# Last feed-forward's gate and up products as seven quarter-block products instead of eight, with GpSimd forming the weight sums

## The chip, the cores and the metric

The kernel runs on one core of a Trainium2 chip. The metric is the device time of one execution in microseconds (us). Five queues work side by side: TensorE (PE in the profile; its weight loads are listed apart as PEld), VectorE (DVE), ScalarE (ACT), GpSimd (POOL) and SyncE (SP), which here only issues transfers. They meet in semaphores.

## What is computed

Two transformer blocks run one after the other over 512 tokens of width 1024, all in float32. The change touches only the last part of the second block, its second feed-forward:

```python
h = modulate(x, norm_g[l, 2], mod[:, 2, 0], mod[:, 2, 1])      # rms norm, gain, shift
x = x + 0.5 * mod[:, 2, 2][:, None, :] * swiglu(h, ffn2_w1[l], ffn2_w3[l], ffn2_w2[l])

def swiglu(h, w1, w3, w2):                                     # 1024 -> 2816 -> 1024
    return (jax.nn.silu(h @ w1) * (h @ w3)) @ w2
```

## The kernel before, in words

Activations lie transposed: a tile is 128 features (partitions) by 512 tokens (columns), so `X` is 8 tiles of the model width and the inner width of 2816 is 22 tiles. A float32 product is made of three products of the shorter type float32r: each operand is split into a high part (a rounded copy, by ScalarE) and a low part (operand minus high part, by VectorE), and TensorE accumulates high x high, high x low and low x high in one bank of PSUM (`split_product`, lines 499 to 501). Every such matmul has its own weight load.

Weights come in chunks of 128 x 1024 (512 KB) in the fixed order of `STREAM`. Chunk n goes through `RAW[n % 3]` (transfer, SP), `HI[n % 3]` (line 1204, ScalarE, semaphore `hi_ready`) and `LO[n % 3]` (line 1693, VectorE, `lo_ready`); TensorE counts `chunk_used` when it is done with one. SP starts the transfer of chunk n+3 when the low part of chunk n is made.

In a feed-forward (`ffn` on each engine) a chunk of gate or up weights is one tile of the inner width: 8 blocks of 128 x 128, 24 matmuls of 512 columns. Tile 0 is computed by `unrooted` from x times gain before the norm's factor is known, and scaled afterwards; tile 1 by `behind`, block by block as the norm's tiles appear (lines 607 to 611); the other 20 tiles are 40 chunks in a row. ScalarE takes the silu of the gate out of PSUM (line 1598), VectorE multiplies it with the up product (line 2404), and the hidden tile is split again (`HIDH`, line 1605; `HIDL`, line 2409). When all 22 hidden tiles are there, the down projection runs: 8 output tiles, each three chunks of 8, 8 and 6 blocks, 528 matmuls in all, each output tile added into `X` by VectorE (line 2464) and stored.

The order on each engine is written out by hand. GpSimd issues transfers and does a few copies earlier in the kernel and has nothing in this stage. Memory of the stage: `HIDH` and `HIDL` take 44 KB per partition each.

Of the kernel before, what the change touches and what calls it, by code (L numbers as in the profile page):

```python
# [15 lines left out]
P = 128  # L16
# [31 lines left out]
def swapped(half):  # L48
# [11 lines left out]
          ("out2", 8), ("up3", 2 * FT), ("down3", 3 * DT))  # L60
# [6 lines left out]
LAST_DOWN = [8, 8, 6]  # L67

# [3 lines left out]
def build(nc, wst, ada, cond_d, xT, cols_d, squares_d, pos1_d, pos2_d, lams_d, out):  # L72
    ctx = ExitStack()
    with ctx:
# [49 lines left out]
        HIDL = at("HIDL", A0 + 44, [P, FT, S], F32R)  # L124

# [121 lines left out]

        UP_FIRST = SQ[:, 0, :]
# [8 lines left out]
        def normed(k, t):  # L257
            return Y2[:] if k == 1 and t == 2 else Y[:, t % 2, :]
# [141 lines left out]
        def _(sp):  # L400
# [19 lines left out]
            repeat(sp, (NCH - 3) // 3, more)  # L420
            for n in range(3 + (NCH - 3) // 3 * 3, NCH):
                sp.wait_ge(sem("lo_ready"), n - 2)
                sp.dma_start(RAW[n % 3][:], wst[n]).then_inc(sem(f"raw{n % 3}"), 16)
# [52 lines left out]


        @block.tensor
        def _(pe):
# [32 lines left out]
            def warm_up(n):  # L512

                pe.wait_ge(sem("warm_set"), 1)
                for _ in range(n):
                    mm(PS[:, 5, :], Y[:, 1, 0:P], Y[:, 1, :], start=True, stop=True)
# [311 lines left out]
            def latent_work():  # L828
# [54 lines left out]
                for j in range(3):  # L883
# [3 lines left out]
                    for r in range(2):  # L887
                        to = bank_for(f"uq{2 * j + r}")
                        ins = split_product(to, w, range(3 * r, 3 * r + 3), range(3), (LQH, LQL))
                        if r:  # L890
                            used(ins)
                        else:
                            ins.then_inc(sem("uq_half"), 1)
# [7 lines left out]
                for m in range(4):  # L901
# [3 lines left out]
                    else:  # L905
                        ins.then_inc(sem("uk_done"), 1)
# [3 lines left out]
                for b in range(NB):  # L910
# [9 lines left out]
                    else:  # L920
                        ins.then_inc(sem("uv_done"), 1)
# [237 lines left out]

            warm_up(3)  # L1160
# [22 lines left out]
            ffn(2, 6)  # L1183
# [3 lines left out]
        def _(act):  # L1187
            A = nc.scalar.activation

            def split_hi(n0, step=0, i=0):  # L1190
# [6 lines left out]
                if step == 0:  # L1197
                    act.wait_ge(sem(f"raw{n0 % 3}"), 16 * (n0 // 3 + 1))
# [31 lines left out]
            def load_roots():  # L1230

                A(SM[:, 85:86], EPSC, ACT.Sqrt).then_inc(sem("table_loaded"), 1)

            def stds(k):
                if k == 4:
                    act.wait_ge(sem("fused_sums"), 2)
                    A(FSTD[:, 0:4], FV[:, 0:4], ACT.Sqrt, bias=EPS2C, scale=1.0 / D).then_inc(sem("fused_std"), 1)
# [8 lines left out]
            def high(k, t):  # L1246
# [8 lines left out]
                else:  # L1255
                    shift = 3 * g * DT + t
                    A(oh[:, t, :], Y[:, t % 2, :], ACT.Identity, bias=MOD[:, shift:shift + 1])\
                        .then_inc(sem("split_hi"), 1)

            def norm(k):  # L1260
# [20 lines left out]
                for t in range(nt):  # L1281
# [5 lines left out]
                    if t == 5:  # L1287
                        split_hi(NEXT[k] + 2)

            def unrooted_copy(k, r):  # L1290
# [4 lines left out]
                else:  # L1295
                    A((SILU[0], UP_FIRST)[r], PS[:, r, :], ACT.Copy).then_inc(sem("unrooted_copied"), 1)

            def table(k, tab):

                act.wait_ge(sem("angle"), k + 1)  # L1300
                A(tab[:, 1, :], Y[:, 0, :], ACT.Sin).then_inc(sem("sin"), 1)
# [23 lines left out]
            def project_in2():  # L1325
                n0 = FIRST["in2"]
                for j in range(IN2_STEPS):
                    if j > 2:
                        split_hi(n0 + j)
                    if j == IN2_STEPS - 1:  # L1330

                        A(SM[:, 85:86], EPSC, ACT.Exp).then_inc(sem("table_loaded"), 1)
# [63 lines left out]
            def latent_copies(p):  # L1396
# [12 lines left out]
                if 12 <= p < 18:  # L1409
# [3 lines left out]
                    else:  # L1413
                        act.wait_ge(sem("uq_half"), m // 2 + 1)
# [1288 lines left out]
```

## Time and profile before

| | |
|---|---|
| Time, median of 3 runs | 1868.12 us (1867.55 to 1869.95) |
| Span of the profiled execution, first to last instruction | 1863.9 us |
| TensorE matmul records / weight load records | 1855.8 us / 1488.2 us |
| VectorE / ScalarE / GpSimd busy | 1071.2 / 742.6 / 60.0 us |
| Last feed-forward, after its norm, to the end | 1523 to 1864 us |

The profiled execution is given by its span alone; the runs' times also hold what lies before its first and after its last instruction, and their median is 4.2 us above it. A matmul's record runs from its start to its last result, and records of neighbours overlap, so TensorE's sum of records says only that it has no pauses; what one matmul costs is the distance between two starts.

### The profile page before, as it was taken

The page shows a single profiled execution, that of the slowest core. Times are in us where ns is not written, and L with a number is a line of the kernel's source. Part 1 is how long each engine was busy: PE and PEld are TensorE (multiplying, and loading weights), DVE is VectorE, ACT ScalarE, POOL GpSimd, SP SyncE. Part 2 cuts the span into 40 slices and gives each one's busy share as a digit, 9 for nine tenths or more (in the row PEclk, how much of TensorE's full clock was granted, in tenths as well). Part 3 has the DMA queues.
Part 4 walks back from the last instruction along what each step waited for, and adds up shares of the span by engine and source line. Part 5 has one row for each costly group of instructions (what it writes and reads, how often), then busy time and mean ns, then how long its engine had stood idle before and what let it go on. Part 6 is the DMA issues. An engine that isn't in the chain of part 4 may idle for free.

```text
span 1863.9 us, 24687 instructions
## 1 busy us (share of the span) xinstructions
PE 1855.8 (100%) x8814; PEld 1488.2 (80%) x8816; DVE 1071.2 (57%) x1755; ACT 742.6 (40%) x1251; POOL 60.0 (3%) x104
## 2 busy tenths in 40 slices
PE   9999999999999999999999999999999999999999
PEld 7777778888888888888888888767768888888887
DVE  7777456757666566733334457867785773333332
ACT  6465445442223233432323334456555452232221
POOL 0001000001111000000000010100000000000000
PEclk9999999999999999999999999999999999999999
DMA  5212213447777563333232332211112333333332
GB/s 187 90 57 68 66 59 121 135 140 227 233 217 226 186 207 111 91 98 101 90 101 91 113 102 91 81 57 54 50 57 68 102 91 102 91 100 97 96 112 90
DMA packets 58285, 207.71 MB, mean 111 GB/s; under 512 B 6688, under 2 KB 6816, under 8 KB 58208
## 3 DMA queue, kind: packets, MB, share of 16 engines
q1 hardware_dynamic: 47232, 167.67, 28.6%
q0 software_dynamic: 10976, 39.00, 6.7%
q8 instruction: 50, 0.82, 0.2%
q14 instruction: 27, 0.22, 0.0%
HBM read 204.48 MB, written 2.10 MB: 111 GB/s over the span
## 4 chain that ended last, share of the span: by engine, by line
PE 97%; DVE 2%; issue 1%; ACT 0%; DVEq 0%; ACTq 0%
PE PS L499 27%; PE PS L501 27%; PE PS L500 27%; PE PS L996 2%; PE PS L1036 2%; PE PS L1023 1%; PE PS L607 1%; PE PS L608 1%; PE PS L611 1%; PE PS L535 1%; PE PS L652 1%; PE PS L539 1%; PE PS L536 1%; PE PS L943 1%; PE PS L768 1%
## 5 line engine op out<-in xcount | busy, mean ns | idle before, releaser
L1693 DVE TENSOR_TENSOR LO<-RAW,HI 128x1024 fp32r<-128x1024 f32 x309 | 377.9, 1223 | 396.3 <-ACT HI L1204 394.4
L499 PE MATMUL PS<-XH,HI 128*128 128x512 f32 x1424 | 561.9, 395 | 0.0
L501 PE MATMUL PS<-XH,LO 128*128 128x512 f32 x1424 | 554.9, 390 | 0.0
L500 PE MATMUL PS<-XL,HI 128*128 128x512 f32 x1424 | 554.4, 389 | 0.0
L1204 ACT ACTIVATE HI<-RAW 128x1024 fp32r<-128x1024 f32 x309 | 326.6, 1058 | 521.7 <-PE PS L501 507.1
L499 PEld LDWEIGHTS PS<-XH,HI 128*128 128x128 f32 x1424 | 267.3, 188 | 61.6 <-issue 7.8
L501 PEld LDWEIGHTS PS<-XH,LO 128*128 128x128 f32 x1424 | 267.3, 188 | 56.9
L500 PEld LDWEIGHTS PS<-XL,HI 128*128 128x128 f32 x1424 | 267.5, 188 | 53.4
L499 PE MATMUL PS<-HIDH,HI 128*128 128x512 f32 x528 | 205.4, 389 | 0.0
L500 PE MATMUL PS<-HIDL,HI 128*128 128x512 f32 x528 | 205.4, 389 | 0.0
L501 PE MATMUL PS<-HIDH,LO 128*128 128x512 f32 x528 | 205.4, 389 | 0.0
L500 PEld LDWEIGHTS PS<-HIDL,HI 128*128 128x128 f32 x528 | 99.1, 188 | 20.7
L501 PEld LDWEIGHTS PS<-HIDH,LO 128*128 128x128 f32 x528 | 99.1, 188 | 20.6
L499 PEld LDWEIGHTS PS<-HIDH,HI 128*128 128x128 f32 x528 | 99.1, 188 | 20.5
L1874 DVE SCALAR_TENSOR_TENSOR ADA<-ADA,COND 128x1024 f32<-128x1024 f32 x72 | 87.8, 1220 | 20.8 <-DMA ADA<-ada 20.4
L2404 DVE TENSOR_TENSOR Y<-T,PS 128x512 f32<-128x512 f32 x43 | 29.6, 689 | 82.1 <-PE PS L501 82.1
L2223 DVE TENSOR_REDUCE SM<-PS 128x1 f32<-128x128 f32 (+3 forms) x96 | 43.8, 487 | 31.8 <-issue 15.5
L1598 ACT ACTIVATE T<-PS 128x512 f32<-128x512 f32 x28 | 16.7, 597 | 96.4 <-PE PS L501 96.4
L1605 ACT ACTIVATE HIDH<-Y 128x512 f32 (+1 forms) x66 | 41.7, 632 | 22.9 <-DVE Y L2404 21.1
L1510 ACT ACTIVATE P<-PS,SM 128x128 f32<-128x128 f32 (+3 forms) x64 | 33.2, 524 | 43.5 <-DVE SM L2223 43.4
L499 PE MATMUL PS<-MH,HI 128*128 128x512 f32 x128 | 49.8, 389 | 0.0
L500 PE MATMUL PS<-ML,HI 128*128 128x512 f32 x128 | 49.8, 389 | 0.0
(408 smaller groups left out, 2123.9 us busy)
## 6 DMA issues: line engine op xcount, KB each, us to landing
RAW<-weights SPq DMA_DIRECT2D x309, 512.0 KB, 3.5
ADA<-ada POOLq DMA_DIRECT2D x72, 512.0 KB, 4.6
y_out<-X SPq DMA_DIRECT2D x8, 256.0 KB, 4.7
X<-x_in SPq DMA_DIRECT2D x3, 512.0 KB, 7.4
RAW<-weights SPq DMA_DIRECT2D x4, 256.0 KB, 5.2
X<-x_in SPq DMA_DIRECT2D x2, 256.0 KB, 4.0
COND<-condition POOLq DMA_DIRECT2D x1, 512.0 KB, 4.7
SQC<-squares SPq DMA_DIRECT2D x1, 320.0 KB, 8.5
```

The lines of the kernel that those rows point to most:

```text
L499: mm(bank, a, moving[0][:, t, :], start=start, stop=False)
L500: mm(bank, a, moving[1][:, t, :], start=False, stop=False)
L501: ins = mm(bank, z, moving[0][:, t, :], start=False, stop=stop)
L996: mm(PS[:, score_bank(a, u), 0:n], at_["q"](2 * p + r, i), at_["k"](2 * p + r, n), start=True, stop=False)
L1036: ins = mm(PS[64 * r:64 * r + 64, 5 + g % 2, k * P:(k + 1) * P], ATT[a]["v"](kb, 2 * p + r), ATT[a]["PT"][2 * (t % 2) + r][:, kb * P:(kb + ...
L1204: A(HI[n0 % 3][:], RAW[n0 % 3][:], ACT.Copy).then_inc(sem("hi_ready"), 1)
L1510: A(at_["P"][u % 3][:, 0:n], PS[:, score_bank(a, u), 0:n], ACT.Exp, bias=NMX[:, u % 4:u % 4 + 1], accum_out=RSU[:, u % 4:u % 4 + 1]).then_ ...
L1605: A(HIDH[:, bass.ds(t, 1), :], Y[:, 0:1, :], ACT.Copy).then_inc(sem("hid_hi"), 1)
L1693: V.tensor_tensor(LO[n0 % 3][:], RAW[n0 % 3][:], HI[n0 % 3][:].bitcast(F32), ALU.subtract)\
L1874: V.scalar_tensor_tensor(out=ADA[j][:], in0=ADA[j][:], scalar=1.0, in1=COND[:], op0=ALU.mult, op1=ALU.mult, accum_out=MOD[:, bass.ds(step ...
L2223: V.tensor_reduce(NMX[:, u % 4:u % 4 + 1], PS[:, score_bank(a, u), 0:n], AX, ALU.max, negate=True)\
L2404: V.tensor_tensor(Y[:, 0, :], SILU[j % 3], PS[:, 2 * (j % 3) + 1, :], ALU.mult)\
```

## The change

**Products.** Twenty pairs replace the 40 chunks: an even pair p holds the gate weights of two inner tiles, an odd one the up weights of the same two. A pair's weights are a 2 x 2 block matrix (contraction halves by the two tiles: a11, a12, a21, a22, each 128 x 512 in memory), the normed tokens are one as well (feature tiles 0 to 3 and 4 to 7 by tokens 0 to 255, `EARLY`, and 256 to 511, `LATE`). Instead of eight products of quarter blocks there are seven (the form with four weight sums and four token sums): `A11 A12 S1 S2 S4 S3 A22`, each 4 blocks x 3 = 12 matmuls of 256 columns. The order is `A11 A12` of pair 0 and then for every p: `S1 S2 S4 A11(p+1) S3 A12(p+1) A22`. Products are accumulated on each other in PSUM where the scheme allows it (S2 on A11's bank, S4 on S1's, S3 and A22 on A11's); three intermediate results per pair are copied out by ScalarE and three added by VectorE.

**Weights.** The pairs' weights go to a new ring of two buffers (`SRAW`, two transfers of 512 KB each). GpSimd makes the four sums S1 = a21 + a22, S2 = S1 - a11, S4 = a12 - S2, S3 = a11 - a21 into `SB`. Each of the seven forms (512 columns) is split into high and low parts in the old `HI` and `LO` buffers, four products ahead; two forms that are neighbours in one buffer and ready together are split by one instruction of 1024 columns, others singly.

**Tokens.** Four sums T1 to T4 of the normed tokens (1024 columns each) and their high and low parts are made once, by GpSimd, VectorE and ScalarE together, at the start of the stage.

**Order.** The inner width is worked off in three parts of 8, 8 and 6 tiles (6, 8 and 6 pairs), each followed by its share of the down projection over all 8 output tiles, added into `X` every time. In the last part the last product stands behind the first blocks of the down projection. Tile 0's scaling and tile 1's product on VectorE and ScalarE are moved in between the products.

**Queues.** While TensorE works on product s, ScalarE and VectorE each go through one step, in this order. `after_product(s - 1)`: ScalarE copies the result of A11, S1 or S2 (and takes the silu of A22's in an even pair); VectorE adds to the result of A12, S4 or S3 and in an odd pair multiplies with the silu. `ahead_hi` and `ahead_lo`: the high and the low part of a form four products ahead. `later`: silu of the sums in an even pair, the hidden tile's high or low part in an odd one.

**Elsewhere.** Some semaphores are merged or dropped to make room (`uq_half`, `uk_done`, `uv_done` become `latent_part`; table loads and half copies no longer increment anything).

```diff
-          ("out2", 8), ("up3", 2 * FT), ("down3", 3 * DT))
+          ("out2", 8), ("up3", 4), ("fa3", 22), ("da3", 8), ("fb3", 28), ("db3", 8), ("fc3", 20), ("dc3", 8))
+def _products():
+    order = [("A11", 0), ("A12", 0)]
+    for p in range(NPAIRS):
+        order += [("S1", p), ("S2", p), ("S4", p)]
+        order += [("A11", p + 1)] * (p + 1 < NPAIRS) + [("S3", p)]
+        order += [("A12", p + 1)] * (p + 1 < NPAIRS) + [("A22", p)]
+    return order
...
SP
+            def pair(p, m):
+                if p < 2:
+                    sp.wait_ge(sem("branch_scaled"), 2 * DT)
+                else:
+                    sp.wait_ge(sem("s_made"), 4 * p - 4)
+                    sp.wait_ge(*low_made("A22" if m else "A12", p - 2))
+                sp.dma_start(SRAW[p % 2][:, m, :], wst[real_pair(p, m)]).then_inc(sem(f"sraw{p % 2}{m}"), 16)
...
GpSimd
+            def sums_of(p):
+                w = SRAW[p % 2]
+                a11, a12, a21, a22 = w[:, 0, 0:S], w[:, 0, S:2 * S], w[:, 1, 0:S], w[:, 1, S:2 * S]
+                pool.wait_ge(sem(f"sraw{p % 2}1"), 16 * (p // 2 + 1))
+                if p:
+                    pool.wait_ge(*low_made("S1", p - 1))
+                pool.tensor_tensor(SB[:, 0, :], a21, a22, ALU.add).then_inc(sem("s_made"), 1)
...
+                pool.tensor_tensor(SB[:, 1, :], SB[:, 0, :], a11, ALU.subtract).then_inc(sem("s_made"), 1)
...
+                pool.tensor_tensor(SB[:, 2, :], a12, SB[:, 1, :], ALU.subtract).then_inc(sem("s_made"), 1)
...
+                pool.tensor_tensor(SB[:, 3, :], a11, a21, ALU.subtract).then_inc(sem("s_made"), 1)
+            def token_sums():
+                pool.wait_ge(sem("normed"), NDB[6] + 4)
+                pool.tensor_tensor(T1[:], YA[:, :, LATE], YA[:, :, EARLY], ALU.subtract).then_inc(sem("pool_tokens"), 1)
+                pool.wait_ge(sem("high_tokens"), 1)
+                pool.tensor_tensor(TL[:, 0], T1[:], TH[:, 0].bitcast(F32), ALU.subtract).then_inc(sem("pool_tokens"), 1)
+                pool.wait_ge(sem("split_lo"), SPLIT_TB[7])
+                pool.tensor_tensor(T4, YC[:, :, EARLY], YC[:, :, LATE], ALU.subtract).then_inc(sem("pool_tokens"), 1)
+                pool.wait_ge(sem("pool_tokens"), 3)
+                pool.tensor_tensor(T4, T4, T1[:], ALU.add).then_inc(sem("pool_tokens"), 1)
...
TensorE
+                def product(s):
+                    kind, p = PRODUCTS[s]
+                    v, h = divmod(s, 2)
+                    pe.wait_ge(*low_made(kind, p))
...
+                    elif kind == "S4":
+                        pe.wait_ge(sem("p5_copied"), p + 1)
+                    elif kind == "S3":
+                        pe.wait_ge(sem("u_copied"), p + 1)
+                    elif kind == "A22":
+                        pe.wait_ge(sem("c22_made"), p + 1)
...
+                    for t in range(4):
+                        a, z = hi[:, t * P:(t + 1) * P], lo[:, t * P:(t + 1) * P]
+                        mm(bank, a, xh[:, t, :], start=opens and t == 0, stop=False, skip_group_check=True)
+                        mm(bank, a, xl[:, t, :], start=False, stop=False, skip_group_check=True)
+                        ins = mm(bank, z, xh[:, t, :], start=False, stop=t == 3, skip_group_check=True)
+                    ins.then_inc(sem("chunk_used" if h else "half_done"), 1)
...
ScalarE, while TensorE works on product s
+                        if s > 2 * v0:
+                            after_product(s - 1)
+                        ahead_hi(v_chunk(2, s // 2), (s % 2,))
+                        if s > 2 * v0 + 1:
+                            later(s - 2)
...
VectorE, while TensorE works on product s
+                        if s > 2 * v0:
+                            after_product(s - 1)
+                        ahead_lo(v_chunk(2, s // 2), (s % 2,))
+                        if s > 2 * v0 + 2:
+                            later(s - 3)
...
+                elif kind == "S3":
+                    v.wait_ge(*product_done(kind, p))
+                    v.wait_ge(sem("p5_copied"), p + 1)
+                    V.tensor_tensor(dst[1][:, LATE], P5C, bank, ALU.add).then_inc(sem("c22_made"), 1)
```

## Rows read from the trace of the kernel before

**Rows 1.** The page: span, and busy time of each engine.

```profile
span 1863.9 us, 24687 instructions
...
PE 1855.8 (100%) x8814; PEld 1488.2 (80%) x8816; DVE 1071.2 (57%) x1755; ACT 742.6 (40%) x1251; POOL 60.0 (3%) x104
```

**Rows 2.** Busy time by stretch: gate and up chunks, then down projection.

```profile
core 0: us, PE busy (x) PEld busy (x) DVE busy (x) ACT busy (x) POOL busy (x), PEclk, DMA share, GB/s
...
1523.00:1743.00 220.00, 220.00 (x972) 182.19 (x971) 78.64 (x85) 66.85 (x86) 0.00 (x0) 1.00 0.32 100
1743.00:1863.00 120.00, 117.65 (x520) 97.08 (x518) 33.07 (x31) 22.60 (x22) 0.00 (x0) 1.00 0.32 101
```

**Rows 3.** Timeline inside a gate or up chunk: start, length, instruction.

```profile
1650.14 0.39 PE L501 MATMUL PS<-XH,LO 128*128 128x512 f32 x1
1650.15 0.19 PEld L499 LDWEIGHTS PS<-XH,HI 128*128 128x128 f32 x1
1650.37 0.39 PE L499 MATMUL PS<-XH,HI 128*128 128x512 f32 x1
...
1653.77 0.39 PE L499 MATMUL PS<-XH,HI 128*128 128x512 f32 x1
```

**Rows 4.** Groups by shape: float32r matmuls of 512 and 256 columns.

```profile
L1002 PE MATMUL PS<-KS,QS 4*128 4x512 f32 x8 | 2.0, 496 | 0.0
...
L1002 PE MATMUL PS<-KS,QS 4*128 4x256 f32 x8 | 1.5, 380 | 0.0
```

**Rows 5.** Timeline of a run of short matmuls, and the stage's weight loads (group).

```profile
97.50 0.97 PEld L972 LDWEIGHTS PS<-DV,PT 128*128 128x128 f32 x8
97.61 1.05 PE L972 MATMUL PS<-DV,PT 128*128 128x128 f32 x8
...
L499 PEld LDWEIGHTS PS<-XH,HI 128*128 128x128 f32 x320 | 60.1, 188 | 12.6
```

**Rows 6.** Groups by shape: of the stage, and two 256-column ones elsewhere.

```profile
L499 PE MATMUL PS<-XH,HI 128*128 128x512 f32 x320 | 124.5, 389 | 0.0
...
L1693 DVE TENSOR_TENSOR LO<-RAW,HI 128x1024 fp32r<-128x1024 f32 x67 | 82.1, 1226 | 143.7 <-ACT HI L1204 143.4
L1204 ACT ACTIVATE HI<-RAW 128x1024 fp32r<-128x1024 f32 x66 | 69.7, 1057 | 158.8 <-PE PS L501 155.3 <-PE PS L539 3.5
...
L2409 DVE TENSOR_TENSOR HIDL<-Y,HIDH 128x512 f32 x18 | 12.3, 685 | 0.0
L1605 ACT ACTIVATE HIDH<-Y 128x512 f32 x18 | 11.4, 633 | 0.0
...
L2464 DVE SCALAR_TENSOR_TENSOR X<-PS,MOD,X 128x512 f32<-128x512 f32 x4 | 3.0, 752 | 17.7 <-PE PS L501 17.7
...
L2299 DVE TENSOR_TENSOR X<-X,PS 128x256 f32<-128x256 f32 x2 | 0.8, 419 | 1.8 <-PE PS L501 1.8
...
L1519 ACT ACTIVATE PT<-PS 128x256 f32<-128x256 f32 x24 | 7.8, 385 | 0.0
```

**Rows 7.** GpSimd's copies (durations, then timeline) and VectorE beside them.

```profile
L447 POOL COPY KM<-KR x8: 603/607/1600, 146.7 to 151.8; 32x512 f32<-32x512 f32 x8
...
146.70 5.68 POOL L447 COPY KM<-KR 32x512 f32<-32x512 f32 x8 [131.78 <-DVE LKL L1832]
147.50 1.44 DVE L1693 TENSOR_TENSOR LO<-RAW,HI 128x1024 fp32r<-128x1024 f32 x1 [0.95 <-ACT HI L1204]
...
151.91 1.02 DVE L1887 TENSOR_TENSOR T<-Y,TAB_P 128x512 f32<-128x512 f32 x1
```

**Rows 8.** Timeline at the end of the last norm and after the last result.

```profile
1518.89 1.63 DVE L1828 SCALAR_TENSOR_TENSOR XL<-Y,MOD,XH 128x512 fp32r<-128x512 f32 x2
...
1522.76 0.62 PE L611 MATMUL PS<-XL,HI 128*128 128x512 f32 x2
...
1860.26 0.39 PE L501 MATMUL PS<-HIDH,LO 128*128 128x512 f32 x1
1860.69 0.75 DVE L2464 SCALAR_TENSOR_TENSOR X<-PS,MOD,X 128x512 f32<-128x512 f32 x1 [12.58 <-PE PS L501]
```

**Rows 9.** The page, transfers: size of one and time to landing.

```profile
RAW<-weights SPq DMA_DIRECT2D x309, 512.0 KB, 3.5
```

More of the change, by code:

```diff
@@ L67, with v_chunk, real_chunk, real_pair @@
 LAST_DOWN = [8, 8, 6]
+NPAIRS = 20
+def _products():
[5 more added lines that the diff above has]
+    return order
+PRODUCTS = _products()
+PRODUCT_AT = {form: s for s, form in enumerate(PRODUCTS)}
+NV = len(PRODUCTS) // 2
+PARTS = ((0, 22), (22, 50), (50, 70))
+PART_NAMES = "abc"
+PART_TILES = ((0, 8), (8, 16), (16, 22))
+TOGETHER = [PRODUCTS[2 * v:2 * v + 2] == [("A11", 0), ("A12", 0)] or
+            PRODUCTS[2 * v][0] + PRODUCTS[2 * v + 1][0] in ("S1S2", "S2S4") for v in range(NV)]
+APART = np.cumsum([0] + [not t for t in TOGETHER]).tolist()
+HID_ORDER = [2, 3, 0, 4, 5, 1] + list(range(6, FT))
+HID_COUNT = {t: k + 1 for k, t in enumerate(HID_ORDER)}
+def v_chunk(f, v):
+    part = sum(v >= p[0] for p in PARTS) - 1
+    return FIRST[f"f{PART_NAMES[part]}{f + 1}"] + v - PARTS[part][0]
+V_OF = {v_chunk(2, v): v for v in range(NV)}
+ORDINARY = [n for n in range(NCH) if n not in V_OF]
+RAW_COUNT = {n: sum(m <= n and m % 3 == n % 3 for m in ORDINARY) for n in ORDINARY}
+RAW_BEFORE = {n: max([m for m in ORDINARY if m < n and m % 3 == n % 3], default=None) for n in ORDINARY}
+REAL = FIRST["up3"]
+def real_chunk(n):
+    for part, name in enumerate(PART_NAMES):
+        first = FIRST[f"d{name}3"]
+        if first <= n < first + DT:
+            return REAL + 2 * FT + DT * part + n - first
+    return n
+def real_pair(p, m):
+    return REAL + 4 + 2 * p + m
 KB = 1024
@@ new lines, in product_bank, with form, form_made @@
+        def product_bank(kind, p):
+            return BANK_B if kind == "A12" else (BANK_C if kind in ("S1", "S4") else BANK_A)[p % 2]
+        def form(kind, p):
+            if kind in S_SLOT:
+                return SB[:, S_SLOT[kind], :]
+            return SRAW[p % 2][:, kind == "A22", {"A11": 0, "A12": S, "A22": S}[kind]:{"A11": S, "A12": 2 * S, "A22": 2 * S}[kind]]
+        def form_made(kind, p):
+            if kind in S_SLOT:
+                return sem("s_made"), 4 * p + S_SLOT[kind] + 1
+            return sem(f"sraw{p % 2}{int(kind == 'A22')}"), 16 * (p // 2 + 1)
@@ new lines, in later @@
+            def later(s):
+                kind, p = PRODUCTS[s]
+                if p % 2 == 0 and kind == "A12":
+                    act.wait_ge(sem("c11_made"), p + 1)
+                    A(G[0][:, EARLY], G[0][:, EARLY], ACT.Silu).then_inc(sem("part_silu"), 1)
+                elif p % 2 == 0 and kind == "S4":
+                    act.wait_ge(sem("c12_made"), p + 1)
+                    A(G[0][:, LATE], G[0][:, LATE], ACT.Silu).then_inc(sem("part_silu"), 1)
+                elif p % 2 == 0 and kind == "S3":
+                    act.wait_ge(sem("c22_made"), p + 1)
+                    A(G[1][:, LATE], G[1][:, LATE], ACT.Silu).then_inc(sem("part_silu"), 1)
+                elif p % 2 and kind in ("S4", "A22"):
+                    m = int(kind == "A22")
+                    hidden_hi(pair_tile(p, m), H[m])
@@ L1799, in norm @@
                         split_lo(NEXT[k] + 1)
+                    if k == 6 and t == 6:
+                        forms_lo(0)
                 lo(k, nt - 1)
@@ L2578, in _ffn, with _ffn_by_pairs @@
         chunks += [_tile(w[0:1024]), _tile(w[1024:2048]), _tile(w[2048:FF])]
+    return chunks
+def _ffn_by_pairs(gate, up, down):
+    g, u = _tiles(gate), _tiles(up)
+    chunks = [g[0], u[0], g[1], u[1]]
+    for t in range(2, FT, 2):
+        chunks += [g[t], g[t + 1], u[t], u[t + 1]]
+    for t0, t1 in PART_TILES:
+        chunks += [_tile(down[t0 * P:t1 * P, m * P:(m + 1) * P]) for m in range(DT)]
     return chunks
```

405 lines of the change are left out of this document (370 added, 35 removed).

## The prediction

> **What bounds the kernel now.** I read the busy shares first: TensorE's matmuls cover the whole span, while VectorE, ScalarE and GpSimd have room [rows 1]. Then I read the stretches of the stage that is changed. From 1523 us, when the normed tokens are ready, to 1743 us run the 40 remaining gate and up chunks, and from there to 1863 us the down projection. TensorE is at 100% and 98% with the granted clock at 1.00, VectorE at 36% and 28%, and GpSimd does nothing [rows 2]. Last I read single instructions: sixteen starts lie between 1650.14 and 1653.77 us, so a 512-column matmul comes every 0.2269 us, each with a weight load of its own that starts with the matmul in front of it [rows 3]. The matmul record of 0.39 us is start to last result, not its price. The price is the pitch. Forty chunks x 24 matmuls x 0.2269 = 217.8 us, which is the stretch of 220 us. So only a change in what TensorE streams, or a new wait of TensorE, moves the end.
>
> **What is removed and added on TensorE.** Removed: those 960 matmuls of 512 columns (the chain counts 320 of each of three kinds [rows 6]). Added: 20 pairs x 7 products x 12 matmuls = 1680 of 256 columns. The four chunks of gate and up of tiles 0 and 1 and all 528 matmuls of the down projection stay. The columns fall by 1/8, but the weight loads rise from 960 to 1680, each now under half as long a matmul. The price of a 256-column float32r matmul is not in the trace as a stream. Two rows bound it. Records of float32r matmuls of 256 and 512 columns last 380 and 496 ns [rows 4]; the difference, 116 ns, less about 3 for rounding (0.2269 / 2 = 0.1134), says that time goes by columns. Were part of the 0.2269 fixed (the excess over 512 columns at 2.4 GHz, 13.5 ns), it would be 0.120. For the load: eight loads of 128x128 in front of 128-column matmuls take 0.97 us, the last record 0.19, so (0.97 - 0.19) / 7 = 0.111 us each, although one record is 0.19 [rows 5]. Loads therefore overlap one another and can follow at 0.111. The larger of 0.1134 and 0.111 counts; with hardly any margin I take 0.114. A product is then 1.37 us, a pair 9.58 us, and the 1680 cost 191.5 us. **Gain before waits: 217.8 - 191.5 = 26.3 us.**
>
> **Load on the other engines, per pair of 9.58 us** [rows 6]. Each of the seven products needs its own 512-column weight form split. One pair of forms per pair of tiles is split as a whole 1024 columns, five singly. VectorE: 1.23 + 5 x 0.69 = 4.7 us for the low parts, three 256-column additions on PSUM at 0.42 = 1.3; an odd pair (up) adds four products of 0.42 and two low parts of 0.69 = 3.1. That is 5.9 us in an even and 9.0 in an odd pair, mean 7.5. ScalarE: 1.06 + 5 x 0.63 = 4.2 for the high parts, three copies of 0.385 from PSUM = 1.2, and 1.3 to 1.7 for silu or the hidden tile's high part: 6.8. GpSimd: four sums of 512 columns with two SBUF inputs, which nothing in this trace shows. The nearest row is its one-input copy of 512 columns, 0.607 us [rows 7]. Below that it can't be; twice the copy, 1.2, is my value, because a second stream of the same length must come in; the far end is 1.6, the copy that was held up. That makes 4.8 us per pair (2.4 to 6.4). On mean load TensorE remains the bound.
>
> **Waits that the new order makes.** Most hand-overs have two or more products of 1.37 us between: the high and low parts are made four products ahead, the banks of A11, A12 and S1 come free a pair earlier. Two have only one product of slack: S4 behind the copy of S1's result, and A22 behind the addition that reads S3's result (`c22_made`). The second misses in every even pair. Count from the end of A11 of pair p+1: its result is visible 0.2 us later (the record outlasts the pitch by 0.16, and VectorE started 0.04 after such an end [rows 8]). ScalarE copies it (0.385) and only then makes the joint high part of S2 and S4 of the next pair (1.06): 1.65. VectorE's joint low part (1.23) stands in its queue in front of the addition: 2.9; the addition (0.42): 3.35; the first load of A22 0.1 more: 3.45. TensorE gets there after S3 and A12, 2 x 1.37 = 2.74. So it waits 0.7 us, ten times: 7 us. In odd pairs no split stands there and the addition is done 0.6 us after S3. What queues behind VectorE in this wait is the sum of A12 and the next low part, both with slack.
>
> **GpSimd beside VectorE.** [Rows 7] show what they do to each other. Of eight GpSimd copies six took 0.607 us, and the one that began under VectorE's split (147.50 to 148.94) took 1.60: it waited for the end of the split and then took its 0.607. The split took 1.44 instead of 1.23, and a VectorE product of two SBUF operands at 151.91, under the last copy, 1.02 instead of 0.69. The page "SBUF — State Buffer" of the Trainium skill (section "Who interferes with whom") says the same: one lock, held for a whole instruction, between GpSimd and VectorE instructions with two SBUF inputs; the second rival below is that rule taken in full. By the rows, then, the two add up: two-input VectorE work is 4.7 us in even and 7.3 in odd pairs, mean 6.0, plus 4.8 is 10.8 us against 9.58. But the records include set-up that need not hold anything (the split lost 0.21 us to a copy of 0.607), so I count a collision at half, and see where the sums fall: those of pair p+2 start when its second load has landed, 3.5 us after A22's low part of pair p [rows 9], that is shortly after the tight addition, and have gone by the next one. They mostly eat slack. I add 0.15 us per pair, 3 us; bounds 0 and 20 x (10.8 - 9.58) = 24. The page "GPSIMD Engine Reference" of the Trainium skill (section 3.1) gives a two-input add of 2048 columns as 4497 ns, a quarter of which is 1.12 us; by that the sums are 4.5 us per pair and the lock 10.5. It warns against elementwise work on this engine; no run here has timed one yet.
>
> **The start.** Before, VectorE ended the norm at 1520.5 and TensorE needed the last low part at 1522.76 [rows 8], a margin of 2.2 us. Now one weight split (1.23) stands in front of the last two low parts and GpSimd's first token sums (1024 columns, 2.4 us each) run beside it: about 1 us late. Behind it VectorE has four 256-column operations for T2 (4 x 0.48), the joint split, a half split and T2's low part (1.23), 5 to 8 us with GpSimd's sums for T4 beside it, against S2 due 4.1 us after TensorE's last old matmul: 1 to 3 us. T3's parts are 5.75 us of VectorE later, S3 is due 5.5 us after S2: 0.5 to 1.5. Together 2.5 to 5.5; I take 4.5.
>
> **What costs nothing.** The three parts of the down projection: same 528 matmuls; the 16 more additions into X (0.75 us) lie beside 24 matmuls of 5.4 us; at a seam TensorE has seven of eight blocks (4.8 us) for the last hidden tile's 0.42 + 0.63 + 0.69. Were that cover gone it would be 1.9 us a seam. Loads: 68 chunks as before, 3.5 us each against a chunk's 5.4 or a pair's 9.6; SP holds later loads behind `branch_scaled`, in front of an out projection of 8 x 5.4 us. Merged semaphores and dropped increments free nothing on the path.
>
> **Sum.** -26.3 + 7 (even pairs) + 3 (GpSimd) + 4.5 (start) = -11.8 us. The profiled execution spans 1863.9 us, so it would become 1852.1; the runs' median lies 4.2 us above the span (what is around it), which gives 1856.3.
>
> **Rivals.**
> - *All is hidden.* GpSimd and the split order find slack, the start costs 2: 1868.1 - 24 = 1844. For it: the mean loads. Against: the 0.7 us count, which has no free term. 0.17.
> - *The lock sets the pace (other side).* VectorE's two-input work and GpSimd's sums exclude each other, 10.8 us per pair, and with every collision paid by VectorE (7.5 + 4.8, less 0.5 that overlaps PSUM work) 11.8. 20 pairs: +24 to +44 over 191.5, with the start -26.3 + 4.5: +3 to +22, so 1871 to 1890. It decides from a pair of 10.7 us on. For it: [rows 7]. Against: the sums' place in the order. 0.20.
> - *A fixed part per matmul.* Pitch 0.120: +10 us, 1866, no change. Against it the two record lengths. 0.09.
> - *Weight loads bound.* If a float32r load can't overlap the next one, each matmul costs its 0.188 us [rows 5]: 1680 x 0.188 = 316 us, 1868 + 98 = 1966. The Trainium skill's first page, "Trainium Kernel Development and Optimization" (section "Best Practices"), tells one to judge the distance to the roofline by the share of weight loads, not of matmuls; here that share is 83% in the stage, so by that rule more loads are the wrong trade. The 0.111 us stream of [rows 5] speaks against it. 0.04.
>
> My forecast as worked out has 0.50, its own range 1851 to 1861. Faster by over 0.2% (3.7 us; about what a measurement tells from no change): 0.50 + 0.17 + a rest of the lock case that stays mild, 0.70. Within it: 0.12. Slower: 0.18. The range takes in the hidden case and the mild end of the lock: 1843 to 1873.
>
> **What the changed profile would show.** Pitch: starts 0.113 to 0.115 apart inside a product. Even pairs: TensorE idle 0.5 to 0.9 us in front of A22, released by the addition. GpSimd: sums of 1.2 us, some near 2 or more, VectorE's half splits over 0.69 where they meet. Start: waits of 1 to 3 us in front of S2 and S3 of pair 0. The forecast is wrong if the pitch is above 0.118, if pairs take over 10.3 us, or if the waits in front of A22 are missing.

## The result: 13 us slower, where 12 us faster was forecast

The kernel after takes 1881.29 us (median of 4 runs, 1878.81 to 1882.92), the kernel before 1867.87 us beside it. The ratio is 1.0069, 95% interval 1.0054 to 1.0083. That is slower by 13.4 us, outside the predicted range of 1843 to 1873. The profiled execution after spans 1881.1 us against 1863.9 [rows 1]; 3 us of these 17 lie in code that is the same in both (last section). Two of the three signs by which the forecast said it would be wrong are there: a pitch above 0.118 us, and pairs of over 10.3 us.

The page of the kernel after, busy time of each engine:

```profile
PE 1852.6 (98%) x9536; PEld 1519.7 (81%) x9536; DVE 1219.0 (65%) x1942; ACT 805.6 (43%) x1414; POOL 193.6 (10%) x188
```

TensorE is busy about as long as before and the span is longer: it now waits. Busy time by stretch, of the kernel after; the first row is the start of the stage, the others steady parts:

```profile
core 0: us, PE busy (x) PEld busy (x) DVE busy (x) ACT busy (x) POOL busy (x), PEclk, DMA share, GB/s
1525.00:1550.00 25.00, 16.82 (x99) 15.58 (x100) 24.26 (x25) 11.73 (x19) 15.41 (x8) 0.82 0.17 63
1550.00:1575.00 25.00, 22.62 (x184) 22.45 (x184) 21.77 (x28) 14.37 (x28) 11.05 (x9) 0.97 0.23 85
1675.00:1700.00 25.00, 24.43 (x204) 24.26 (x203) 24.57 (x31) 14.16 (x29) 14.91 (x10) 1.00 0.28 106
1700.00:1725.00 25.00, 24.01 (x200) 23.84 (x199) 24.57 (x27) 15.06 (x30) 16.09 (x11) 1.00 0.23 85
```

VectorE, at 36% in [rows 2], is at 98%, and TensorE is not at 100% any more. In the first stretch TensorE works two thirds of the time, with the granted clock at 0.82 on average. Timeline of TensorE after, the pitch inside a product, and then starts that it waited for (in brackets how long, and for what):

```profile
1691.05 0.28 PE L1403 MATMUL PS<-XL,HI 128*128 128x256 f32 x1
1691.16 0.28 PE L1404 MATMUL PS<-XH,LO 128*128 128x256 f32 x1
...
1692.01 0.28 PE L1402 MATMUL PS<-XH,HI 128*128 128x256 f32 x1
...
1526.94 0.50 PE L813 MATMUL PS<-XL,HI 128*128 128x512 f32 x1 [1.99 <-DVE XL L2225]
1573.94 0.36 PE L1402 MATMUL PS<-TH,HI 128*128 128x256 f32 x1 [2.38 <-DVE SQ L2961]
1599.71 0.56 PE L1402 MATMUL PS<-TH,HI 128*128 128x256 f32 x1 [3.91 <-DVE SQ L2961]
1707.91 0.35 PE L1402 MATMUL PS<-TH,HI 128*128 128x256 f32 x1 [0.99 <-DVE SQ L2961]
```

The waits of TensorE after, 1500 to 1860 us, by what ended them (us in total, times, longest):

```profile
PE PS L1402 <- DVE SQ L2961: 10.9, 9, 3.9
PE PS L1402 <- DVE TL L2927: 4.8, 1, 4.8
PE PS L813 <- DVE XL L2225: 2.0, 1, 2.0
PE PS L1402 <- DVE LO L2891: 1.3, 1, 1.3
```

From 1691.05 to 1692.01 are eight matmuls: the pitch is 0.120, not 0.114. L2961 is the c22 addition; the forecast had A22 wait 0.7 us for it in every even pair. The nine waits stand in those pairs, but two of them, in the first part, are 2.4 and 3.9 us. The other three are the start: the norm's last low part, the joint low part of S1 and S2 of pair 0, and T3's low part, 8.1 us together. (A bracket counts from the end of the record before it, 0.28 us long where the pitch is 0.120. So each wait costs about 0.16 us more than its bracket says.) Groups by shape, 1675 to 1725 us, after (mean ns of one behind the busy time):

```profile
L2897 DVE TENSOR_TENSOR LO<-SRAW,HI 128x512 fp32r<-128x512 f32 x15 | 24.1, 1629 | 0.1
L2897 DVE TENSOR_TENSOR LO<-SB,HI 128x512 fp32r<-128x512 f32 x10 | 10.6, 1058 | 0.6 <-ACT HI L1600 0.6
L2891 DVE TENSOR_TENSOR LO<-SB,HI 128x1024 fp32r<-128x1024 f32 x4 | 4.9, 1214 | 0.0
L2944 DVE TENSOR_TENSOR SQ<-RB,PS 128x256 f32<-128x256 f32 x3 | 1.2, 412 | 0.0
```

The low part of 512 columns takes 1.63 and 1.06 us instead of 0.685 [rows 6]. The one of 1024 columns, and additions with one input in PSUM, keep their length. Timeline of VectorE and GpSimd after, around one such pair:

```profile
1701.27 3.49 DVE L2897 TENSOR_TENSOR LO<-SRAW,HI 128x512 fp32r<-128x512 f32 x2
...
1706.22 1.21 DVE L2891 TENSOR_TENSOR LO<-SB,HI 128x1024 fp32r<-128x1024 f32 x1
1707.36 0.41 DVE L2961 TENSOR_TENSOR SQ<-RB,PS 128x256 f32<-128x256 f32 x1
...
1700.94 1.57 POOL L657 TENSOR_TENSOR SB<-SRAW,SB 128x512 f32<-128x512 f32 x1
1702.47 1.75 POOL L660 TENSOR_TENSOR SB<-SRAW 128x512 f32<-128x512 f32 x1
```

Two low parts took 3.49 us where two sums ran. The sums take 1.5 to 1.8 here, not 1.2; in the whole stage the shortest take 1.28, and what lies above that is most likely time in which VectorE held GpSimd. And the joint low part (1706.22) stands directly ahead of the addition that A22 waits for. The addition comes at 1685.99, 1707.36 and 1728.72: 10.68 us a pair, against 7 x 12 x 0.120 = 10.08 of matmuls and the 9.58 forecast.

### The profile page after: what moved, and what is told of

It is laid out like the page before. It is cut to its first block, busy times and chain, and to the rows that moved or that the text cites. A ratio compares the mean times of both kernels' runs of the same rounds, so it can differ in the third digit from the quotient of the medians.

```text
span 1881.1 us, 26501 instructions
## 1 busy us (share of the span) xinstructions
PE 1852.6 (98%) x9536; PEld 1519.7 (81%) x9536; DVE 1219.0 (65%) x1942; ACT 805.6 (43%) x1414; POOL 193.6 (10%) x188
## 4 chain that ended last, share of the span: by engine, by line
PE 89%; DVE 7%; issue 2%; ACT 1%; DMA 0%; SPq 0%; DVEq 0%; ACTq 0%
PE PS L701 23%; PE PS L703 22%; PE PS L702 22%; DVE LO L2897 2%; PE PS L1198 2%; PE PS L1402 2%; PE PS L1403 2%; PE PS L1404 2%; PE PS L1238 2%; PE PS L1225 1%; PE PS L809 1%; PE PS L810 1%; PE PS L813 1%; DVE HL L2933 1%; PE PS L854 1%
## 5 line engine op out<-in xcount | busy, mean ns | idle before, releaser
L701 PE MATMUL PS<-XH,HI 128*128 128x512 f32 x1104 | 437.8, 397 | 0.0
L703 PE MATMUL PS<-XH,LO 128*128 128x512 f32 x1104 | 430.7, 390 | 0.0
L702 PE MATMUL PS<-XL,HI 128*128 128x512 f32 x1104 | 430.3, 390 | 0.0
L701 PE MATMUL PS<-HIDH,HI 128*128 128x512 f32 x352 | 137.1, 389 | 0.0
L703 PE MATMUL PS<-HIDH,LO 128*128 128x512 f32 x352 | 137.1, 389 | 0.0
L702 PE MATMUL PS<-HIDL,HI 128*128 128x512 f32 x352 | 137.0, 389 | 0.0
L1402 PE MATMUL PS<-TH,HI 128*128 128x256 f32 x320 | 93.5, 292 | 17.1 <-DVE SQ L2961 10.9
L1403 PE MATMUL PS<-TL,HI 128*128 128x256 f32 x320 | 92.4, 289 | 0.0
L1404 PE MATMUL PS<-TH,LO 128*128 128x256 f32 x320 | 92.4, 289 | 0.0
L2897 DVE TENSOR_TENSOR LO<-SRAW,HI 128x512 fp32r<-128x512 f32 x58 | 75.2, 1313 | 7.9 <-ACT HI L1600 7.8
L702 PEld LDWEIGHTS PS<-HIDL,HI 128*128 128x128 f32 x352 | 66.1, 188 | 13.5
```

What stands on the lines that cost most here:

```text
L701: mm(bank, a, moving[0][:, t, :], start=start, stop=False)
L702: mm(bank, a, moving[1][:, t, :], start=False, stop=False)
L703: ins = mm(bank, z, moving[0][:, t, :], start=False, stop=stop)
L1402: mm(bank, a, xh[:, t, :], start=opens and t == 0, stop=False, skip_group_check=True)
L1403: mm(bank, a, xl[:, t, :], start=False, stop=False, skip_group_check=True)
L1404: ins = mm(bank, z, xh[:, t, :], start=False, stop=t == 3, skip_group_check=True)
```

## The experiments

All times are medians beside runs of the kernel before on the same chip (1867.7 to 1868.7 us).

**The pitch alone** (probe_pitch). The kernel before, with streams behind its last result:

```
+for n in (128, 192, 256, 320, 384, 448, 512):
+    for i in range(48):
+        w = HI[i % 2][:, (i // 2 % 8) * P:(i // 2 % 8 + 1) * P]
+        mm(PS[:, 5, 0:n], w, XH[:, i % 8, 0:n], start=i == 0, stop=i == 47, ...)
```

> The kernel before, and behind its last result seven streams of 48 float32r matmuls each, moving 128, 192, 256, 320, 384, 448 and 512 columns of one tile against changing 128-column weights, with nothing else running. The profile of after has 256-column matmuls 0.120 us apart, where I had taken 0.114. If each matmul pays a fixed 13.5 ns beside its columns at 2.4 GHz, the starts are 0.147 us apart at 320 columns, 0.1735 at 384, 0.200 at 448 and 0.227 at 512, and below 256 columns the weight load of 0.11 us sets the pace. If time goes by columns alone (0.2269 at 512), 256 gives 0.113, 320 gives 0.142, 384 gives 0.170, and the 0.120 of after came from its two-engine traffic. If weight loads hold 256 columns at 0.120, then 128, 192 and 256 columns all show 0.120 and 320 shows 0.142.

Timeline of TensorE in this run, asked from different moments on; each row is what is left of the streams, from its start, with the count of matmuls left:

```profile
1866.74 51.43 PE L1188 MATMUL PS<-XH,HI 128*128 128x128 f32 x323
1869.76 48.42 PE L1188 MATMUL PS<-XH,HI 128*128 128x128 f32 x296
1873.81 44.37 PE L1188 MATMUL PS<-XH,HI 128*128 128x192 f32 x260
1875.81 42.36 PE L1188 MATMUL PS<-XH,HI 128*128 128x192 f32 x242
1877.60 40.57 PE L1188 MATMUL PS<-XH,HI 128*128 128x256 f32 x227
1881.32 36.85 PE L1188 MATMUL PS<-XH,HI 128*128 128x256 f32 x196
1889.02 29.15 PE L1188 MATMUL PS<-XH,HI 128*128 128x384 f32 x143
1891.28 26.89 PE L1188 MATMUL PS<-XH,HI 128*128 128x384 f32 x130
1907.79 10.38 PE L1188 MATMUL PS<-XH,HI 128*128 128x512 f32 x45
1915.74 2.43 PE L1188 MATMUL PS<-XH,HI 128*128 128x512 f32 x10
```

From 1877.60 to 1881.32 are 31 matmuls of 256 columns: 0.120 us each. In the same way 384 columns take 2.26 / 13 = 0.174, 512 take 7.95 / 35 = 0.227, 192 take 2.00 / 18 = 0.111, and 128 take 3.02 / 27 = 0.112. So from 256 columns on a fixed 13 to 14 ns stands beside the columns, with nothing else running. That 128 and 192 columns cost the same is what a bound by the weight loads looks like, at the 0.111 of [rows 5]; it lies below the 0.120. (448 columns came out at 0.207 where the line gives 0.200; that is left open.)

**GpSimd's sums almost gone** (no_sums). The four sums of a pair cover 8 columns: `pool.tensor_tensor(SB[:, 0, 0:8], a21[:, 0:8], a22[:, 0:8], ALU.add)`, and so on. The forms, and so the products, are then not those of the reference.

> The changed kernel, but GpSimd's four sums of each pair cover 8 of their 512 columns (the forms S1 to S4 are then a constant set once, so the gate and up products are not the reference's); the token sums, all waits, all splits and all products stay. Lock theory (GpSimd's two-input sums stretch VectorE's two-input operations on SBUF, and the waits of A22 for the c22 addition come from that): the 128x512 low parts fall from 1.31 and 0.97 us to 0.7, the 128x1024 ones likewise, the waits of A22 behind the first two pairs go, a pair takes 10.1 us instead of 10.68, and the time is 1864 to 1870 us. Rival, the order alone (c22 stands behind the joint low part on VectorE, whose length hardly matters): 1877 to 1881 us, with A22 still 0.5 us late in every even pair. Rival, the start alone (the token sums): the time stays within 2 us of 1881.

1867.92 us, ratio 0.9999 (0.9990 to 1.0009): all of the loss is gone. Groups by shape, 1675 to 1725 us:

```profile
L2899 DVE TENSOR_TENSOR LO<-SRAW,HI 128x512 fp32r<-128x512 f32 x14 | 9.6, 689 | 8.0 <-ACT HI L1602 8.0
L2899 DVE TENSOR_TENSOR LO<-SB,HI 128x512 fp32r<-128x512 f32 x8 | 5.5, 690 | 3.1 <-ACT HI L1602 3.1
```

Busy time by stretch, in the order of columns as above:

```profile
1675.00:1700.00 25.00, 24.77 (x207) 24.60 (x206) 16.88 (x29) 15.12 (x31) 2.81 (x9) 1.00 0.25 91
```

The low parts are back at 0.69 and VectorE's busy time falls from 24.6 to 16.9 of 25 us. So in the kernel after nearly 8 of its 25 us were time in which it was held back. Over four whole pairs (from one c22 addition to the fourth after it) it is busy 41.86 us after and 27.92 here: 16 sums of 1.28 us or more held it 13.9 us, 0.87 each.

Two pairs take 20.61 us here, not 21.37. The joint low part still stands ahead of the c22 addition, so this run also shows what the order costs by itself. Timeline of TensorE, one of seven such starts in the steady part:

```profile
1692.10 0.36 PE L1404 MATMUL PS<-TH,HI 128*128 128x256 f32 x1 [0.23 <-DVE SQ L2963]
```

The nine waits for this addition are 3.1 us together, against 10.9 in the kernel after.

**Copies instead of sums** (sums_as_copies). `pool.tensor_copy(SB[:, 0, :], a21)`, and so on, with all 512 columns.

> The changed kernel, but each of GpSimd's four sums of a pair is a copy of its first input, of the same 512 columns (the forms are then not those of the reference); the token sums stay. If any GpSimd access to SBUF holds VectorE back, a 128x512 low part stays above 1 us and the time is 1876 us or more. If it is two-input operations on both engines that exclude each other, low parts fall to 0.69 us as in no_sums and the time is 1866 to 1871 us.

1868.69 us, 1.0002 (0.9993 to 1.0012). Groups by shape, 1620 to 1830 us:

```profile
L2897 DVE TENSOR_TENSOR LO<-SRAW,HI 128x512 fp32r<-128x512 f32 x40 | 31.0, 774 | 19.3 <-ACT HI L1600 19.3
...
L648 POOL COPY SB<-SRAW 128x512 f32<-128x512 f32 x13 | 10.3, 793 | 147.1 <-DVE LO L2891 86.7 <-DMA SRAW<-weights 60.4
```

A copy still adds 0.09 us to a low part on the mean, and single low parts that met one took up to 1.10 us. So one-input work isn't free of the lock either, but a copy alone is half as long as a sum (0.61 against 1.28), and the slack takes it. My alternative "any access" asked for low parts above 1 us and a time of 1876 us or more; as a price it fell, as a mechanism it did not. The run can't tell whether it is the second input or only the length that hurts.

**The sums on VectorE** (sums_on_vector), for pairs 2 to 19; what is undone is where they are made:

```
+kind, p = PRODUCTS[s]
+if 2 <= p + 1 < NPAIRS:
+    for k in {"S1": (0,), "S2": (1, 2), "S4": (3,)}.get(kind, ()):
+        sum_of(k, p + 1)          # V.tensor_tensor into SB[:, k, :]
```

> The changed kernel with the weight sums of pairs 2 to 19 on VectorE (behind the steps of S1, S2 and S4 of the pair before); GpSimd keeps those of pairs 0 and 1 and the token sums. Without sums VectorE was busy 16.9 of 25 us in the steady part (no_sums); four more operations of some 0.68 us a pair make it 23.5 of 25. Lock theory: a low part of 128x512 is back at 0.69 us, two pairs take 20.6 us instead of 21.4, and the time is 1869 to 1874 us. Rival (VectorE is now full, in order, and the c22 and c11 additions come late all the same): two pairs take 21 us or more and the time is 1876 to 1886 us.

1874.86 us, 1.0035 (1.0023 to 1.0046), 6 us faster than after. The time lies between the two expectations, 0.9 us above the lock theory's; two pairs take the 20.6 us that it named. Groups by shape, 1620 to 1830 us, one kind of sum, then a steady stretch:

```profile
L2990 DVE TENSOR_TENSOR SB<-SRAW 128x512 f32<-128x512 f32 x26 | 17.8, 684 | 0.0
```

```profile
1675.00:1700.00 25.00, 24.77 (x207) 24.59 (x206) 22.46 (x40) 15.51 (x32) 0.00 (x0) 1.00 0.26 86
```

A sum costs VectorE 0.684 us here. On GpSimd it took 1.5 us and held VectorE for 0.87 on the mean. With four more operations a pair VectorE is busy 22.5 of 25 us and TensorE waits less.

**The order on VectorE** (late_split). The joint low part of S2 and S4 one step later, behind the c22 addition:

```
-if TOGETHER[n_v] and 0 in halves:
+kind = PRODUCTS[2 * n_v][0]
+if TOGETHER[n_v] and (1 if kind == "S2" else 0) in halves:
```

> The changed kernel with one thing moved on VectorE: the joint low part of S2 and S4 of an odd pair stands behind the c22 addition of the even pair ahead of it (step A12) and no longer before it (step S3). Order theory: A22 no longer waits in even pairs, which is worth the 0.6 to 1.0 us of each of ten waits, and more in the first two, with the half clock behind them: 1869 to 1873 us. Lock theory: VectorE is all but full under the lock (24.6 of 25 us), so the time comes back as a wait of S2 or A12 for a low part or the c11 addition: 1877 to 1881 us. If the start is all that costs, no change from 1881.

1875.37 us, 1.0037 (1.0023 to 1.0051). Some 6 us come back, between the two expectations (the order theory had 8 to 12), and nearly all of it in the first part. In the steady part the lock theory holds: the wait of A22 in even pairs is gone, but an odd pair waits in its place, and two pairs still take 21.35 us. Timeline of TensorE, one such start:

```profile
1710.06 0.36 PE L1402 MATMUL PS<-TH,HI 128*128 128x256 f32 x1 [0.69 <-DVE Y L2962]
```

**Both** (vector_late). The sums of pairs 2 to 19 on VectorE and the later joint low part together.

> sums_on_vector and late_split together. If the joint low part ahead of the c22 addition is what is left of the wait of A22 (0.39 us in every other pair without any sums, more with a full VectorE), this is 2 to 4 us faster than sums_on_vector; if not, within 1 us of it. late_split alone was worth 6 us, most of it in the first pairs, and the lock stretched what it moved.

1867.98 us, 0.9996 (0.9986 to 1.0005): 6.9 us faster than the sums on VectorE alone, where I expected 2 to 4. In that one TensorE still waited 1.5 and 2.4 us for the c22 addition in the first part and 0.23 in every second pair behind it; here it waits 0.4 and 0.2 and then never again for it. In the two traces some 5 us of the gain lie in the first part and some 3 behind it, where two pairs now take 20.16 us, the 14 products' own time. Busy time of a steady stretch:

```profile
1675.00:1700.00 25.00, 25.00 (x211) 25.00 (x210) 22.37 (x40) 14.87 (x32) 0.00 (x0) 1.00 0.34 117
```

So nearly all of what is still lost against the matmuls' own time lies in the start, which is untouched here.

**The start, reordered (two tries).** In the first (start_order), on the kernel after, VectorE makes the first forms' low part behind the norm's last, and GpSimd's T4 sums wait for T2 and its sums of pair 1 for T3.

> The changed kernel with the start of the stage put in another order: VectorE makes the low part of the first two forms behind the last two low parts of the norm instead of between them; GpSimd waits for VectorE's T2 before the T4 sums and for VectorE's T3 before the sums of pair 1. Start theory (the tight place is the stage's first 20 us, where GpSimd's long sums stretch VectorE's four T2 and four T3 operations to 5.8 and 4.8 us, and TensorE waits 2.0, 1.3 and 4.8 us and then runs at half clock): the waits fall to some 3 us in all and the time to 1871 to 1876 us. Rival (GpSimd's sums then come late themselves): A22 of pair 0 waits for T4, or A11 for the forms of pair 1, and the time is 1880 to 1885 us. If the lock in the steady part is all, within 2 us of 1881.

1879.89 us, 1.0061 (1.0044 to 1.0078): 1.4 us, no gain to speak of. The four T2 operations fell from 5.82 to 1.67 us, but the T4 sum, now later, met what came next: it took 5.61 us itself (2.36 in the kernel after), and T3 stretched to 3.78. The second try (vector_start) was made on the sums on VectorE:

```
-T3, T4 = YC[:, :, LATE], YC[:, :, EARLY]
+T3, T4 = YA[:, :, EARLY], YC[:, :, EARLY]
...
-order = [("A11", 0), ("A12", 0)]
+order = [("A11", 0), ("A12", 0), ("A11", 1)]
```

> sums_on_vector with the start reordered so that nothing of GpSimd lies beside the norm's last low part or VectorE's T2 and T3: the low part of the first difference on GpSimd behind the norm's last low part, T3 written where the early half of the first normed tiles was (so that it needs no sum of GpSimd first) and made right behind T2, the T4 sums behind T3, T3's high part ahead of T4's on ScalarE, and the product A11 of pair 1 ahead of S1 of pair 0. Start theory: of the 16 us that TensorE lost in the first 20 us of the stage, waits and half clock together, some 8 come back, and the time is 1861 to 1867 us. Rival (T4 or the sums of pair 1 come late on GpSimd instead, as in start_order): within 3 us of sums_on_vector.

1876.53 us, 1.0044 (1.0027 to 1.0061): a miss of the 1861 to 1867 expected, and what the rival had named. TensorE no longer waits for the norm's last low part, but it waits 3.8 us later on, for a copy of ScalarE that stood behind T3's high part. Timeline of VectorE, GpSimd and ScalarE:

```profile
1524.94 2.37 DVE L2910 TENSOR_TENSOR SM<-MOD 128x4 f32<-128x4 f32 x1
...
1524.03 3.26 POOL L668 TENSOR_TENSOR TL<-T,TH 128x1024 fp32r<-128x1024 f32 x1 [6.22 <-DVE XL L2226]
...
1534.11 1.06 ACT L1588 ACTIVATE TH<-YA 128x1024 fp32r<-128x1024 f32 x1 [3.21 <-DVE YA L2920]
```

The first row is VectorE, held 2.37 us over a difference of 4 columns that took 0.16 in the kernel after, while the GpSimd operation of the second row ran. Moving GpSimd's work moves the collision.

**The token sums almost gone** (no_token_sums). Both of the changes above that helped, and GpSimd's four token operations on 8 columns of each 256.

> vector_late (weight sums of pairs 2 to 19 on VectorE, joint low part behind the c22 addition), but GpSimd's four operations on tokens cover 8 columns of each 256 (the token forms S1 and A22 are then not the reference's); a memset gives the rest a value ahead of them. vector_late has no wait of TensorE left behind the first 100 us of the stage, and all its 16 us of lost time lie in the start. If GpSimd's token sums beside VectorE's norm, T2 and T3 make that loss, the wait for the last XL falls below 1 us, those for the low part of S1 and S2 and for T3's low part from 1.3 and 4.8 us to under 3 in all, and the time from 1868 to 1861 to 1864 us. If it is the amount of VectorE's own work there and its order (the low part of the first forms ahead of the norm's last two), the time stays at 1865 us or above.

1859.49 us, 0.9954 (0.9938 to 0.9969): 8.5 us more, and more than the expectation. (Here too the products are not the reference's.) The wait for the norm's last low part is gone; one for T3's low part stays at 3.8 us. Whose doing that is, the T2 and T3 operations of three runs tell. The kernel after, with token sums and weight sums on GpSimd:

```profile
1527.78 5.82 DVE L2913 SCALAR_TENSOR_TENSOR T<-YC,MOD,T 128x256 f32<-128x256 f32 x4
...
1538.70 4.75 DVE L2920 SCALAR_TENSOR_TENSOR YC<-YC,SM,YA 128x256 f32<-128x256 f32 x4
```

With the token sums but nearly no weight sums (no_sums):

```profile
1524.67 5.85 DVE L2915 SCALAR_TENSOR_TENSOR T<-YC,MOD,T 128x256 f32<-128x256 f32 x4
...
1534.86 1.66 DVE L2922 SCALAR_TENSOR_TENSOR YC<-YC,SM,YA 128x256 f32<-128x256 f32 x4
```

With nearly no token sums but the weight sums of pair 1:

```profile
1525.27 1.68 DVE L2918 SCALAR_TENSOR_TENSOR T<-YC,MOD,T 128x256 f32<-128x256 f32 x4
...
1535.26 2.69 DVE L2925 SCALAR_TENSOR_TENSOR YC<-YC,SM,YA 128x256 f32<-128x256 f32 x4
```

The token sums stretch T2, and the weight sums of pair 1 stretch T3. In the last run these sums lie between 1529.2 and 1536.9 us and also stretch T2's low part to 2.32 us and single ones to 1.77 and 1.46. So what is left of the wait for T3 is in large part the same lock and not VectorE's own amount of work; with the weight sums gone instead, it is 1.1 us.

**A version that beats both** (better). The same outputs, with what the runs had shown: sums on VectorE, the joint low part late, a second set of sums so that GpSimd makes those of pairs 0 and 1 before the norm's tiles, A11 of pair 1 ahead of S1, and T4 without GpSimd. As T2 is late tokens plus shift minus T1, T4 is early tokens plus shift minus T2:

```
+V.scalar_tensor_tensor(out=T4[:, t, :], in0=T4[:, t, :], scalar=MOD[:, c:c + 1],
+                       in1=T2[:, t, :], op0=ALU.add, op1=ALU.subtract)
```

> A kernel with the reference's outputs that puts together what the runs say: vector_late, and for the start a second set of sums (so that GpSimd makes those of pairs 0 and 1 before the norm's tiles, where VectorE mostly waits), the low part of the first forms behind the norm's last, T4 as early tokens plus shift minus T2 in one operation on VectorE, T3 in a place of its own, the first difference's low part on VectorE, and A11 of pair 1 ahead of S1 of pair 0. GpSimd is then left with one operation beside VectorE. VectorE's work from the first forms' low part to A22 of pair 0 adds up to some 15 us where TensorE has 11.5 us of products, so TensorE should lose some 4 us there and not the 13 of vector_late: 1857 to 1863 us, faster than the kernel before (1867.9). If the order of the many small steps leaves ScalarE's copies waiting as in vector_start, it comes to 1864 to 1869 us.

1863.3 us (median of 6 runs), 0.9971 (0.9959 to 0.9983), just above the expected 1857 to 1863. In the start GpSimd has one operation left beside VectorE, and the granted clock stays at 1.00 where it was 0.82. TensorE still waits 1.7, 1.1 and 1.5 us there. The early sums seem to have a price of their own: beside those of pair 1, at 1484.8 to 1490.4 us, seven operations of VectorE took 4.63 us instead of 2.67. In the norm behind them TensorE waited 1.81 us for VectorE instead of 0.68, and the granted clock was 0.93 from 1500 to 1525 us instead of 1.00. No run separates the two. Busy time by stretch:

```profile
1525.00:1550.00 25.00, 20.58 (x147) 18.92 (x146) 22.71 (x38) 16.11 (x28) 0.00 (x0) 1.00 0.18 64
```

## Why the prediction was wrong

**Gain before waits (failed by 10 us).** The step that chose a pitch of 0.114, "time goes by columns", is the first that failed. It alone would have made the change a gain of 2 us instead of 12. Both ends had been worked out, 0.1134 and 0.120, and the stream alone gives 0.120. 1680 x 0.120 = 201.6, so the gain is 217.8 - 201.6 = 16.2 us, not 26.3. I had let the difference of two record lengths [rows 4] decide; those eight-matmul groups are no stream, and a record's length is not its pitch, as I had written myself of [rows 3].

**A22 in even pairs (+7: mechanism right, size by luck).** The place, the releaser and the joint low part in front are as counted, in the steady part too. The size is not. The count had no lock in it, and without one (no_sums) a steady wait is 0.23 us by its bracket, 0.39 by the pitch, where 0.7 was forecast; with a product at 1.44 us the same count gives 3.45 - 2.88 = 0.57. With the lock the nine waits were 10.9 us. Moving the joint low part was worth 6 to 7 us (late_split, vector_late), which looks like the forecast 7, but the larger part of it came from two waits in the first part (3.9 and 2.4 us after, 2.4 and 1.5 with the sums on VectorE). Why the order costs more there is not shown.

**GpSimd beside VectorE (+3: failed).** This is, with the start, the step that turned the sign. The length of a sum was nearly right: 1.28 us where nothing holds it, 1.5 on the mean, for the forecast 1.2. What failed is that the sums would "mostly eat slack". A collision had been counted at half of a sum, 0.6 us; a sum held VectorE for 0.87 on the mean, that is 3.5 us of every pair, because more than two thirds of the single low parts met one. The steady pair paid 0.38 us for it (10.68 against 10.30 in no_sums), not 0.15, and the first part more. Moving the sums of pairs 2 to 19 to VectorE gave back 6.4 us, leaving nearly all of them out 13.4 us; the difference lies in the first pairs, where the sums of pair 1 stretch T3 (in no_sums T3's low part is waited for 1.1 us and not 4.8), and in the waits for the c22 addition. The estimate from the Trainium skill's page "GPSIMD Engine Reference" (section 3.1, a quarter of its time for 2048 columns) was 1.12 us for a sum; the measured 1.28 decides.

**The start (+4.5: failed in size).** The places were right (the last low part, then S2's and S3's forms), the amounts were not: 2.0, 1.3 and 4.8 us are 8.1 of waits alone. The four T2 operations, which I had at 4 x 0.48, took 5.82 us, and the four of T3 4.75 where they take 1.66 unheld. GpSimd's token sums did the first; without these the time falls by 8.5. The weight sums of pair 1, which the forecast did not have in the start at all, did the second. And TensorE ran at a granted clock of 0.82 on average from 1525 to 1550 us, behind its waits, for which I had counted nothing.

**What costs nothing (right).** The two seams show waits of 0.2 us in the trace, and no load of weights is among the releasers of TensorE in the stage. In vector_late, with the same three parts, the steady stretches have no wait.

The sum as the runs have it: -16.2, + 6.9 (order), + 6.4 (weight sums of pairs 2 to 19), + 8.5 (token sums) is +5.6. The measured +13.4 is 8 us more. In no_token_sums TensorE still waits 3.8 us for T3's low part, 0.8 for T2's, and 1 us for A22 and at the seams: 5.6 us in six waits, each some 0.16 longer by the pitch. A mean granted clock of 0.93 from 1525 to 1550 us is 1.75 us more, so about 8 in all.

**Of the rivals,** the lock as the pace named the right mechanism: 1871 to 1890 us held the time, and the pair of 10.68 us is at the 10.7 from which it was to decide. That the numbers fit is in part luck. Of the 10.68 us 10.08 are the matmuls' own at the pitch of 0.120, which this rival did not have; without that error the lock would have come out at its lower bound. It came true together with the fixed part per matmul, which had been priced on its own; I gave the two 0.20 and 0.09 and never their sum. The runs agree with the one lock, held for a whole instruction, of the Trainium skill's page "SBUF — State Buffer" (section "Who interferes with whom"), down to the 4-column difference held for 2.37 us; VectorE's additions with an input in PSUM kept their 0.41. The records do not simply add up, though: 6.0 us of two-input work and 4 x 1.28 of sums are 11.1, and a pair took 10.68.

## What to carry to other kernels

Where a change halves the size of an instruction, price it by a stream of that size, or take the fixed part from the full size's own excess over its columns (13.5 ns here, 6 to 11%); on 1680 matmuls that was 10 us. Elementwise work on GpSimd is not free because GpSimd is idle: wherever VectorE has two SBUF inputs, count most of the GpSimd length of each such operation on VectorE's account (here 0.87 us on the mean for a sum of 1.28, where VectorE itself needs 0.68). In an in-order queue, put the short operation that somebody waits for ahead of the long one with slack; that one line was worth 6 to 7 us here.

## What was not expected of the hardware

The granted clock differs from one execution to the next in code that is the same. Busy time by stretch, first the kernel before, then after; in both TensorE had just waited 1.2 us for the same operation:

```profile
749.00:757.00 8.00, 8.00 (x44) 6.78 (x44) 4.27 (x11) 3.40 (x8) 0.00 (x0) 1.00 0.25 77
```

```profile
749.00:757.00 8.00, 8.00 (x30) 6.69 (x29) 3.34 (x10) 1.18 (x4) 0.00 (x0) 0.57 0.21 76
```

At a mean clock of 0.57, near the lower of its two levels (1.2 GHz), 30 matmuls fit where 44 did, and 3 us are lost. It isn't the change's doing: probe_pitch, which is the kernel before in this place, shows 0.57 too, and the version that beats both has it and is faster all the same. Of that version's six runs five took 1862.9 to 1863.5 us at a mean clock of 0.997, and one 1858.75 at 1.000. What decides it is open. So of the 17 us between the two profiled executions 3 are chance, and 14 agree with the medians. Second, a two-input sum of 512 columns on GpSimd took 1.3 us at the least and 1.45 to 1.63 on the mean of each kind, more than twice its copy of 0.61 [rows 7].
